# Cross attention's last two heads: VectorE takes both maxima first, and copies head two's transposes ahead of head three's probabilities

## The reference, cut to what matters

```
q = (h @ wq).reshape(B, T, 4, 256)
k = (m @ wk).reshape(B, M, 4, 256)      # m: the normalized memory, M = 256
v = (m @ wv).reshape(B, M, 4, 256)
s = einsum('bthd,bmhd->bhtm', q, k) * 256 ** -0.5
p = softmax(s, axis=-1)
o = einsum('bhtm,bmhd->bthd', p, v).reshape(B, T, 1024)
return o @ wo
```

## Time and profile before

| | us |
|---|---|
| median of 3 runs | 2759.46 |
| lowest and highest of them | 2758.95 and 2760.47 |
| the profiled execution | 2754.0 |
| its span, first to last instruction | 2752.2 |
| TensorE busy in the span | 2692.2 (98%) |
| VectorE busy | 1267.9 (46%) |
| ScalarE busy | 1016.7 (37%) |

### The profile page before, as it was taken

How to read it: one execution, slowest core, us unless ns; L and a number is a source line. 1 busy time by engine, 2 the same in 40 slices (tenths; PEclk the granted TensorE clock), 3 DMA queues, 4 the chain that set the end, 5 groups by cost and what they waited for, 6 DMA issues and landing times.

```text
span 2752.2 us, 39526 instructions
## 1 busy us (share of the span) xinstructions
PE 2692.2 (98%) x16362; PEld 2349.6 (85%) x16362; DVE 1267.9 (46%) x2178; ACT 1016.7 (37%) x1621; POOL 275.5 (10%) x350
## 2 busy tenths in 40 slices
PE   8999999999999999999999999999999999999997
PEld 7888999999987879788888988888888887888887
DVE  5544654333432323573334533435666654633333
ACT  4545443222332223352223432323566543522222
POOL 0000300001200000220000310012211130300002
PEclk9999999999999999999999999999999999999998
DMA  3111243222111212332222132222322222332220
GB/s 141 54 47 47 78 138 104 91 92 78 47 62 62 92 62 77 100 106 94 92 100 92 65 131 94 85 94 75 108 85 69 77 68 79 94 112 92 100 69 31
DMA packets 67683, 232.94 MB, mean 85 GB/s; under 512 B 9008, under 2 KB 11440, under 8 KB 67120
## 3 DMA queue, kind: packets, MB, share of 16 engines
q1 hardware_dynamic: 67504, 230.41, 25.2%
HBM read 228.25 MB, written 2.10 MB: 84 GB/s over the span
## 4 chain that ended last, share of the span: by engine, by line
PE 88%; DVE 4%; ACT 3%; POOL 2%; issue 2%; DMA 1%; DVEq 0%; SPq 0%; POOLq 0%; ACTq 0%
PE ps L590 77%; PE ps L904 2%; PE ps L1030 1%; PE ps L600 1%; POOL R L2685 1%; PE ps L783 1%; POOL S L2670 1%; PE ps L743 1%; PE ps L891 1%; ACT HT L1265 1%; DVE HT L1927 1%; DVE R L1934 1%; PE ps L610 1%; PE ps L1127 1%; PE ps L623 0%
## 5 line engine op out<-in xcount | busy, mean ns | idle before, releaser
L590 PE MATMUL ps<-XH,WH 128*128 128x264 f32 (+2 forms) x1856 | 537.1, 331 | 12.9 <-DVE XL L2644 7.9
L590 PE MATMUL ps<-XH,LENT 128*128 128x512 f32 (+2 forms) x2096 | 526.5, 341 | 3.3 <-DVE XL L1951 3.2
L590 PE MATMUL ps<-XL,WH 128*128 128x264 f32 (+2 forms) x1856 | 523.2, 324 | 0.0
L590 PE MATMUL ps<-XH,WL 128*128 128x264 f32 (+2 forms) x1856 | 522.5, 324 | 0.0
L590 PE MATMUL ps<-HH,LENT 128*128 128x264 f32 (+2 forms) x2220 | 490.5, 318 | 1.9 <-DVE LENT L1905 1.9
L1905 DVE TENSOR_TENSOR WL<-RAW,WH 128x1024 fp32r<-128x1024 f32 (+1 forms) x232 | 286.3, 1234 | 264.0 <-ACT WH L1234 263.4
L590 PEld LDWEIGHTS ps<-XH,LENT 128*128 128x128 f32 x2096 | 355.7, 189 | 53.4 <-DVE XL L1951 4.5
L590 PEld LDWEIGHTS ps<-HH,LENT 128*128 128x128 f32 x2220 | 361.1, 190 | 32.1 <-DVE LENT L1905 2.3
L590 PEld LDWEIGHTS ps<-XH,WH 128*128 128x128 f32 x1856 | 318.8, 189 | 54.0 <-issue 12.7
L590 PEld LDWEIGHTS ps<-XH,WL 128*128 128x128 f32 x1856 | 318.5, 189 | 28.1
L590 PEld LDWEIGHTS ps<-XL,WH 128*128 128x128 f32 x1856 | 318.8, 189 | 26.7
(11 more groups left out here) (216 smaller groups left out, 2661.3 us busy)
## 6 DMA issues: line engine op xcount, KB each, us to landing
RAW<-in_wf SPq DMA_DIRECT2D x128, 512.0 KB, 3.3
RAW<-in_wr SPq DMA_DIRECT2D x48, 512.0 KB, 3.2
RAW<-in_wg SPq DMA_DIRECT2D x44, 512.0 KB, 3.2
RAW<-in_wu SPq DMA_DIRECT2D x44, 512.0 KB, 3.3
RAW<-in_wd SPq DMA_DIRECT2D x32, 512.0 KB, 3.2
RAW<-in_we SPq DMA_DIRECT2D x24, 512.0 KB, 3.3
RAW<-in_wm SPq DMA_DIRECT2D x24, 512.0 KB, 3.2
RAW<-in_wro SPq DMA_DIRECT2D x16, 512.0 KB, 3.2
```

Of the source, the lines that this page charges most:

```text
L590: mm = e.matmul(o[:, to:to + m], wt, xt[:, k, c0 + a * m:c0 + (a + 1) * m], start=(n == 0 and j == 0), stop=(n == nk - 1 and j == 2))
```

## The change

VectorE's `cross_soft` is cut in two functions: `cross_max` (maximum and its scaling) and `cross_prob` (reciprocal and probabilities). For heads 0 and 1 they are called one behind the other, as before. For heads 2 and 3 the order on VectorE becomes: maxima of 2, maxima of 3, probabilities of 2, the copy of head 2's transposes, probabilities of 3. Before it was: maxima of 2, probabilities of 2, maxima of 3, probabilities of 3, the copy. The lists of the other engines, and the number of instructions, stay as they are.

```
-        def cross_soft(h):
+        def cross_max(h):
             st = cross_cols(h)
             bv = acc(("crs_s", h), 2).rearrange("p (q m) -> p q m", q=4)
             w.wait_ge(*S.score["crs", h])
             e.tensor_reduce(st[:, 0:4], bv, AX.X, ALU.max).then_inc(*S.soft("max", "crs", h))
             w.wait_ge(*S.soft["max", "crs", h])
             e.tensor_scalar(st[:, 4:8], st[:, 0:4], -0.0625, None, ALU.mult).then_inc(*S.soft("neg", "crs", h))
+
+        def cross_prob(h):
+            st = cross_cols(h)
             w.wait_ge(*S.exp["crs", h, 3])
             e.reciprocal(st[:, 12:16], st[:, 8:12]).then_inc(*S.soft("recip", "crs", h))
...
             for h in range(2):
-                cross_soft(h)
+                cross_max(h)
+                cross_prob(h)
...
-            cross_soft(2)
-            cross_soft(3)
+            cross_max(2)
+            cross_max(3)
+            cross_prob(2)
             step(0, 4)
             cross_turn(2)
+            cross_prob(3)
             step(1, 2)
             cross_values(2)
```

## The result

| | kernel before | changed kernel |
|---|---|---|
| median, 15 runs each | 2757.82 us | 2753.17 us |
| lowest to highest | 2754.43 to 2762.19 | 2750.73 to 2757.54 |
| ratio | | 0.9983, 95% interval 0.9975 to 0.9991 |
| the profiled execution | 2754.0 | 2755.86 |
| its span | 2752.2 | 2754.1 |

The profiled execution of the changed kernel, however, is 1.9 us *longer* than that of the kernel before. Both call for an explanation.

What follows compares the result with a forecast made beforehand. TensorE, busy 98% of the span, was taken to bound the kernel. Removing 2.10 us and adding 0.40 gave 1.70 us off, taking the median from 2759.46 to 2757.7 us, range 2755.4 to 2760.6.

Steps and rivals of the forecast that it cites:

- The place and the mechanism: TensorE's values of head 2, waiting for VectorE's late copy: removing the 1.93 us wait gains 2.10 us.
- the transposes are late: Head 2's transposes on TensorE wait for later probabilities: 0.31 to 0.42 us computed, 0.40 taken, bounds 0.3 to 0.6.
- the copy is early: VectorE's copy of head 2's transposes ends at 2304.86, early by 0.35 us, so the values' wait vanishes.
- The sum: Cross attention on TensorE: 2.10 us removed, 0.40 added, 1.70 us off, bounds 1.5 and 1.8.
- The extra cost of a stalled first transpose: Head 2's transposes on TensorE: a stalled first one pays its weight load too, some 0.2 us.
- the level and its spread: Whole kernel: median 5.46 us above the profiled execution, 2759.46 before, 2757.7 after; another set of runs a microsecond away.
- a clock term of zero: TensorE behind the removed wait: clock stayed at 1.00 in the trace; a fall elsewhere took about 1.6 us.
- The larger gain: Rival at head 2's values: removed wait had caused a clock fall, 1.6 us more gain, 2756.1 us, chance 0.1.
- The carry-over to the end: After head 3's values: the wait for GpSimd's sums stays near 2.0 us, so the whole gain reaches the end.
- the prediction's own sign: Trace after the change: a clock below 1.00 in the stretches after 2344 would show the forecast wrong.
- The rival in which a fall of the clock behind that wait gives the gain back: Behind the wait for GpSimd's sums: clock fall priced 1.6 us against 1.7 gain, median 2759.4, chance 0.17.
- "Same" at 0.2%: Whole kernel: every case lies within 0.2%, 5.5 us, of no change; same 0.95, faster 0.04, slower 0.01.

Runs made afterwards that it cites:

- The fourth trace: Kernel before, unedited, profiled and timed again in job 3: mean 2757.63 ± 0.80 us, ratio 0.9999.
- three jobs: Three sets of follow-up runs, each timing the kernel before beside other kernels; kernel before 2757.01 ± 0.18 us, changed kernel 2754.56 ± 0.36 us overall.
- the two with the longest refilled waits: Changed kernel with four or six unused reductions before head 2's copy on VectorE: 2761.46 and 2763.64 us, ratios 1.0016 and 1.0023.

## Why the prediction was right or wrong

**The place and the mechanism: right.** The reductions of head 3 start at 2300.03 (forecast 2300.08), the transposes are late by 0.32 us relative to the scores (0.40 taken, 0.31 the lower computed end), the copy is early, the values of head 2 follow without a wait, head 3's probabilities end at 2306.1 with four microseconds to spare. Two readings of the rows were off without moving the sum: the time between the transposes and the copy was in part VectorE's idle 2.00 us, as shown above, and not all of it work; and of the three loads in the earlier trace rows the second waited as well (until 2323.08), so two loads move with the change, not one. The sum was 1.70 with bounds of 1.5 and 1.8; the traces have 1.84 at the values of head 3 (1.75 at those of head 2, where forecast and trace compare start to start; the eight matmuls behind a wait take 0.07 to 0.08 us longer, which the forecast left out). The extra cost of a stalled first transpose, which I bounded by 0.2, was 0.04.

**The steps that failed: the level and its spread, and a clock term of zero.** The time was worked out as 2759.46 less 1.7, from a median of three runs, and the range allowed another set of runs to sit "a microsecond away". The median of 15 was 2757.82, 1.6 us lower, and over 131 later runs of the same program the standard deviation of one execution is 2.05 us: three runs fix no level to a microsecond. The forecast of 2757.7 against 2753.17 is thus 1.6 us of level and 2.9 us of difference (4.65 against 1.7, with rounding). The range, 2755.4 at its lower end, would have held the first alone (2756.1), but not the second (2754.8), and not both.

In the difference, the step was the clock. The prediction worked out a fall at 1.6 us, found none behind the removed wait in its one trace, and took the likeliest case, no fall, as the size of the effect. But the time of many executions contains the falls of some of them. The fourth trace shows such a fall, at 1.7 us, and over three jobs 0.7 ± 0.3 us of the 2.45 ± 0.40 goes with the clock. The larger gain stood among the rivals with a chance of 0.1 and as all or nothing; what happens in a share of executions belongs in the sum. So does its counterpart, a fall behind the next wait, which the traces show more often after the change than before it; so even the sign of the whole clock term rests on the mean clocks and not on the traces.

**What stays open: the rest of the first result.** Three later jobs gave 1.7, 2.8 and 2.4 us, the first result 4.8 by its means. The 2.3 ± 0.85 us between 4.8 and 2.45 come from both sides: the 15 runs of the kernel before lie 1.4 us above the mean of its 131 later ones, those of the changed kernel 0.9 us below that of its 33. At its mean clock of 0.99213 the line above gives the changed kernel 2754.3 us, against a measured 2753.6 ± 0.5; for those 15 runs of the kernel before no clock is on record. A far draw or something that differed in that set of runs would both do, and no run decides.

**The carry-over to the end: wrong for the single trace, and not shown on average.** I expected the wait for GpSimd's sums to stay near 2.0 us, at 2344.2. It was 3.28 at 2345.28. The prediction had made a constant of one draw, where the four traces of the kernel before have 1.57 to 3.02 us. By the prediction's own sign, a clock below 1.00 in the stretches after 2344, the forecast failed in its first trace. The rival in which a fall of the clock behind that wait gives the gain back did happen in the traces: in all four traces of the changed kernel, but in two of four of the kernel before as well. In twelve traces with a wait of 1.57 to 3.28 us there (the two with the longest refilled waits left aside), the clock fell behind every one of 2.69 us or more and behind none of 2.51 or less; from this line to its last occurrence it took 390.5 to 390.6 us without a fall and 391.9 to 392.1 with one, once 393.4. The clock's 0.7 us in the timed runs points the other way, so that on average the rival doesn't seem to have won.

The Trainium skill's rule (TensorE: Matmul & The Clock Gate, section "What's actually happening"), that the watching block runs freely and so the same program sees its changes of clock in different places, could not be tested by one trace. Four traces of one program agree with the second half of it: the same wait of 1.92 to 1.93 us had a fall behind it once and none three times. That the block runs freely, no run here shows.

**"Same" at 0.2%: right.** 0.17% in the first result and 0.09% by the three jobs (2.45 of 2757) are both within it.

## What to carry to other kernels

A wait of the bounding engine is worth its length and, where falls of its clock follow waits, the price of a fall times the share of executions that have one; give the second term a size even when the trace at hand shows no fall, and do the same for the next wait downstream. A level from three runs is as uncertain as those runs are scattered. For an effect of a few microseconds, measure places of one trace from a common start near the change (here the scores of head 2), and take the net effect from many runs, with the granted clock beside each. When work is moved ahead on one engine, follow all consumers: here half of the copy is on ScalarE, and the maxima's place set when that half could run.

## What the runs showed of the hardware

- One program's executions spread by 2 us (standard deviation), and more than half of the variance goes with the mean granted clock: 1.9 us for each 0.001.
- Equal waits of TensorE, 1.92 to 1.93 us, ended with the clock at 1.00 three times and at 0.57 once, at a price of 1.7 us. Waits of 3.99 and 6.24 us at the same place, in one trace each, both had a fall.
- The first load of 512 KB behind cross attention, 25 us or more after the one before it, took between 3.1 and 5.1 us from its issue to the instruction that uses it, in eight traces of the two kernels.
- VectorE's reciprocal started 0.08 us behind the start of a scaling that takes 0.17 us: with no unmet wait between them, the records of two short instructions overlap by half.
